# A 31-tap convolution shared between four engines: three channel chunks regrouped by token phase and summed on TensorE with block matrices of 16 taps

## What is computed

```python
def conv_mixer(h, w_pw1, b_pw1, w_dw, b_dw, ln_g, ln_b, w_pw2, b_pw2):
    a = h @ w_pw1 + b_pw1
    u = a[..., :D_MODEL] * jax.nn.sigmoid(a[..., D_MODEL:])
    u = causal_depthwise_conv(u, w_dw) + b_dw          # 31 taps, each channel by itself
    u = jax.nn.silu(layernorm(u, ln_g, ln_b))          # mean and variance over the 1024 channels
    return u @ w_pw2 + b_pw2
```

## Time and profile before

| | |
|---|---|
| Median of three executions | 1853.35 us |
| Profiled execution, its own time | 1847.57 us |
| Its span in the profile | 1845.5 us |
| Mean granted TensorE clock | 0.998 of full speed |
| Convolution: end of pw1 on TensorE | 733.3 us |
| Mean product complete, VectorE centres | 781.4 us |

### The profile page before, as it was taken

One profiled execution on the slowest core, in us unless ns is written; L12 is line 12 of the kernel. 1 busy time (PEld: TensorE's weight loads), 2 busy tenths in 40 slices (PEclk: granted clock), 3 DMA queues, 4 the chain that ended last, 5 costly groups with the idle time before them and its releaser, 6 DMA issues.

```text
span 1845.5 us, 20405 instructions
## 1 busy us (share of the span) xinstructions
PE 1803.3 (98%) x8026; PEld 1445.9 (78%) x8026; DVE 811.9 (44%) x1361; ACT 756.0 (41%) x1199; POOL 780.8 (42%) x360
## 2 busy tenths in 40 slices
PE   7999989999999999999999999999999999999998
PEld 6887768888888877478888888877877888767787
DVE  3794442210121179842210121187868841337733
ACT  4523344322242356454322232355546432444533
POOL 3343224444444369924444444344535543433221
PEclk9999999999999999999999999999999999999999
DMA  5232112323333332012333333333323332232111
GB/s 190 81 102 70 58 36 90 102 93 102 92 102 92 92 103 92 12 46 82 102 101 100 94 98 97 103 103 91 103 80 92 103 96 87 76 92 80 47 46 46
DMA packets 100384, 160.32 MB, mean 87 GB/s; under 512 B 7329, under 2 KB 30497, under 8 KB 100289
## 3 DMA queue, kind: packets, MB, share of 16 engines
q1 hardware_dynamic: 100288, 159.02, 28.3%
HBM read 156.90 MB, written 2.10 MB: 86 GB/s over the span
## 4 chain that ended last, share of the span: by engine, by line
PE 92%; DVE 5%; ACT 2%; issue 1%; DMA 0%; SPq 0%; DVEq 0%; ACTq 0%
PE bank L600 27%; PE bank L602 27%; PE bank L601 27%; PE bank L857 2%; PE bank L901 1%; PE bank L1023 1%; PE bank L682 1%; PE bank L1057 1%; ACT prob L1271 1%; PE bank L1042 1%; PE bank L791 1%; ACT spare L1177 1%; DVE rg_u L2033 0%; PE bank L773 0%; PE bank L999 0%
## 5 line engine op out<-in xcount | busy, mean ns | idle before, releaser
L2385 POOL TENSOR_TENSOR w_lo<-w_raw,w_hi 128x1024 fp32r<-128x1024 f32 (+1 forms) x286 | 694.1, 2431 | 1016.0 <-ACT w_hi L1148 1016.0
L1148 ACT ACTIVATE w_hi<-w_raw 128x1024 fp32r<-128x1024 f32 (+1 forms) x286 | 300.5, 1054 | 593.2 <-PE bank L602 587.5
L600 PE MATMUL bank<-x_hi,w_hi 128*128 128x512 f32 (+1 forms) x1264 | 504.0, 399 | 1.2 <-ACT q_feat L1279 0.8
L602 PE MATMUL bank<-x_hi,w_lo 128*128 128x512 f32 (+1 forms) x1264 | 492.5, 390 | 0.0
L601 PE MATMUL bank<-x_lo,w_hi 128*128 128x512 f32 (+1 forms) x1264 | 492.1, 389 | 0.0
L600 PEld LDWEIGHTS bank<-x_hi,w_hi 128*128 128x128 f32 (+1 forms) x1264 | 236.5, 187 | 59.3 <-issue 10.6
L601 PEld LDWEIGHTS bank<-x_lo,w_hi 128*128 128x128 f32 (+1 forms) x1264 | 236.5, 187 | 53.5 <-issue 4.8
L602 PEld LDWEIGHTS bank<-x_hi,w_lo 128*128 128x128 f32 (+1 forms) x1264 | 236.3, 187 | 51.3 <-issue 0.2
L600 PE MATMUL bank<-w_hi,f_hi 128*128 128x512 f32 x512 | 200.0, 391 | 0.0
L602 PE MATMUL bank<-w_hi,f_lo 128*128 128x512 f32 x512 | 199.3, 389 | 0.0
L601 PE MATMUL bank<-w_lo,f_hi 128*128 128x512 f32 x512 | 199.2, 389 | 0.0
(11 more groups left out here) (298 smaller groups left out, 2124.7 us busy)
## 6 DMA issues: line engine op xcount, KB each, us to landing
w_raw<-in_mlp_w SPq DMA_DIRECT2D x128, 512.0 KB, 3.7
w_raw<-in_even_w_in SPq DMA_DIRECT2D x48, 512.0 KB, 3.8
w_raw<-in_dsa_w_in SPq DMA_DIRECT2D x28, 512.0 KB, 3.6
w_raw<-in_odd_w_in SPq DMA_DIRECT2D x24, 512.0 KB, 3.6
w_raw<-in_conv_w_pw SPq DMA_DIRECT2D x32, 256.0 KB, 3.0
w_raw<-in_even_w_out SPq DMA_DIRECT2D x16, 512.0 KB, 3.8
w_raw<-in_dsa_w_out SPq DMA_DIRECT2D x8, 512.0 KB, 3.8
w_raw<-in_conv_w_pw SPq DMA_DIRECT2D x8, 512.0 KB, 3.8
```

What stands on the lines that cost most here:

```text
L600: e.matmul(o, sh, mh, start=first, stop=False)
L602: m = e.matmul(o, sl, mh, start=False, stop=last)
L1148: e.activation(hi, src, ACT.Copy).then_inc(*w_hi.up(u))
L2385: e.tensor_tensor(lo, src, hi.bitcast(F32), ALU.subtract).then_inc(*w_lo.up(u))
```

## The change

Chunks 4, 5 and 6 are now convolved on TensorE in another form, and no diagonals are made.
- **Phases.** For these chunks VectorE writes u ordered by phase: tokens 0, 4, 8, ... first, then 1, 5, 9, ... SP copies 32 channels of one phase at a time within SBUF, so that one tile (`u4`) has 32 channels in 4 phases on its 128 partitions and 128 columns of tokens: 16 DMAs a chunk of 32 partitions by 512 bytes.
- **Block matrices.** `toep` holds for each of the 12 groups (3 chunks by 4 groups of 32 channels) nine matrices of 128x128. A matrix joins 4 input phases to 4 output phases: 16 taps of one channel block. They are products of two broadcast operands, 1152 elements wide: the mask of equal channels and the shifted weights (`lag_w`). VectorE builds eight (five during the first MLP, three ahead of step 0 of pw1), GpSimd four (steps 0 and 1).
- **TensorE.** A group is nine float32 matmuls of 128 columns into bank 6 or 7 in turn, copied with the bias by ScalarE. These copies stand behind all of its products for chunk 1 and a table load. SP brings each group back by four DMAs into `cc`, still ordered by phase.
- **The others.** VectorE has chunks 0, 2, 3 and 7 whole (124 taps); 7 is split over both sums, as 0 is. GpSimd keeps chunk 1 and then sums chunks 0 to 3 into one tile, so that the mean is five matmuls: chunks 4 and 5, the sum, 7, and 6 last. Readers of chunks 4 to 6 put the tokens back in order by strides.
- **Small loads.** 20 DMAs after the load of the units for q0 bring shifted weights, biases and the mask. A memset at the start clears `lag_w`.

```diff
-PE_TAPS = {6: CONV_TAPS[14:], 7: CONV_TAPS}
-POOL_TAPS = {1: CONV_TAPS, 3: CONV_TAPS[12:]}
-DVE_TAPS = {0: CONV_TAPS, 2: CONV_TAPS, 3: CONV_TAPS[:12], 4: CONV_TAPS, 5: CONV_TAPS, 6: CONV_TAPS[:14]}
+PE_CHUNKS = [4, 5, 6]
+PHASES = 4
+BLOCK = P // PHASES
+SHIFTS = (CONV_W - 1 + PHASES - 1) // PHASES + 1
+PH_LEN = S // PHASES
+PE_GROUPS = [(k, g) for k in PE_CHUNKS for g in range(PHASES)]
+TOEP_POOL = [(4, g) for g in range(PHASES)]
+TOEP_EARLY = [(6, 0), (6, 1), (6, 2), (6, 3), (5, 3)]
+TOEP_DVE = TOEP_EARLY + [(5, 0), (5, 1), (5, 2)]
+POOL_TAPS = {1: CONV_TAPS}
+DVE_TAPS = {0: CONV_TAPS, 2: CONV_TAPS, 3: CONV_TAPS, 7: CONV_TAPS}
-MEAN_ORDER = [0, 2, 1, 4, 5, 6, 3, 7]
+MEAN_ORDER = [0, 2, 1, 3, 4, 5, 7, 6]
...
+        def build_toeplitz(e, k, g):
+            n = PE_CHUNKS.index(k)
+            return e.tensor_tensor(toep[:, n, g], same_ch[:, :].unsqueeze(1).broadcast_to([P, SHIFTS * PHASES, BLOCK]),
+                                   lag_w[:, n, g].unsqueeze(2).broadcast_to([P, SHIFTS * PHASES, BLOCK]), ALU.mult)
```

TensorE's program after pw1:

```diff
-            for k, b in TAP_BANK.items():
+            for k, g in PE_GROUPS:
+                b, n = PHASE_BANKS[g % 2], PE_CHUNKS.index(k)
                 empty(b)
+                w.wait_ge(*phases_in(k))
+                w.wait_ge(*(part_added if (k, g) in TOEP_POOL else dve_tapped).at(k, g))
+                for d in range(SHIFTS):
+                    m = e.matmul(bank[b][:, 0:PH_LEN], toep[:, n, g, d * PHASES:(d + 1) * PHASES, :],
+                                 u4[:, n, g, d:d + PH_LEN], start=d == 0, stop=d == SHIFTS - 1)
+                m.then_inc(*mean_mm.up(k, g))
+                free[b] = cent_sq.at(k, g)
```

ScalarE's, behind the products and the table load:

```diff
+            for k, g in PE_GROUPS:
+                w.wait_ge(*mean_mm.at(k, g))
+                e.activation(cu[:, k, g * PH_LEN:(g + 1) * PH_LEN], bank[PHASE_BANKS[g % 2]][:, 0:PH_LEN], ACT.Identity,
+                             bias=ph_bias[:, g, k - PE_CHUNKS[0]:k - PE_CHUNKS[0] + 1]).then_inc(*cent_sq.up(k, g))
```

SP's queue:

```diff
             up_to("pw10")
             load_gain_row("b_pw2")
+            for n, k in enumerate(PE_CHUNKS):
+                load_to(UNITS[f"pw1{k + 1}"][0] + AHEAD + RAW + 2)
+                w.wait_ge(*u_out.at(k))
+                if n:
+                    w.wait_ge(*phases_in(k - 1))
+                for g in range(PHASES):
+                    for i in range(PHASES):
+                        e.dma_start(u4[i * BLOCK:(i + 1) * BLOCK, n, g, SHIFTS - 1:],
+                                    cu[g * BLOCK:(g + 1) * BLOCK, k, i * PH_LEN:(i + 1) * PH_LEN]
+                                    ).then_inc(*turned_in[0].up("phases", k, PHASES * g + i))
+            w.wait_ge(*phases_in(6))
+            for k, g in PE_GROUPS:
+                if (k, g) == (6, 0):
+                    w.wait_ge(*back_in(4))
+                w.wait_ge(*cent_sq.at(k, g))
+                for j in range(PHASES):
+                    to = PHASES - 1 - j
+                    e.dma_start(cc[g * BLOCK:(g + 1) * BLOCK, k, to * PH_LEN:(to + 1) * PH_LEN],
+                                cu[j * BLOCK:(j + 1) * BLOCK, k, g * PH_LEN:(g + 1) * PH_LEN]).then_inc(*turned_in[k == 5].up("back", k, PHASES * g + j))
```

GpSimd's, behind the adds for chunk 1:

```diff
+            w.wait_ge(*dve_tapped.at(2))
+            e.tensor_tensor(csum[:, :], cc[:, 0, :], cc[:, 2, :], ALU.add).then_inc(*part_added.up("sum", 2))
...
+            e.tensor_tensor(csum[:, :], csum[:, :], cc[:, 1, :], ALU.add).then_inc(*part_added.up("sum", 1))
...
+            e.tensor_tensor(csum[:, :], csum[:, :], cc[:, 3, :], ALU.add).then_inc(*part_added.up("sum", 3))
```

More of the change, by code:

```diff
@@ L470, in build, with phases_in, back_in @@
         part_out = signal("conv_product_made", [(k, i) for k in POOL_TAPS for i in POOL_TAPS[k]])
-        part_added = signal("conv_product_added", POOL_ADDS)
-        diag_out = signal("conv_diag_made", [(k, i) for k in PE_TAPS for i in PE_TAPS[k]])
-        pe_tapped = signal("conv_taps_product", [6, 7])
-        dve_tapped = signal("conv_taps_summed", [0, 3, 2, 4, 5, 6])
-        act_tapped = signal("conv_taps_copied", [7])
-        mean_mm = signal("conv_mean_product", ["mean", "var"])
+        lag_in = signal("conv_lags_landed", range(PHASES * (len(PE_CHUNKS) + 2)), 16)
+        part_added = signal("conv_made_on_gpsimd", TOEP_POOL + POOL_ADDS + [("sum", 2), ("sum", 1), ("sum", 3)])
+        dve_tapped = signal("conv_toeplitz_then_taps_made", TOEP_DVE + [0, 2, 3, 7])
+        turned_in = [signal(f"conv_turned_landed{n}",
+                            [(w, k, i) for w, k in keys for i in range(PHASES * PHASES)], 16)
+                     for n, keys in enumerate(([("phases", k) for k in PE_CHUNKS] + [("back", 4), ("back", 6)], [("back", 5)]))]
+        def phases_in(k):
+            return turned_in[0].at("phases", k, PHASES * PHASES - 1)
+        def back_in(k):
+            return turned_in[k == 5].at("back", k, PHASES * PHASES - 1)
+        mean_mm = signal("conv_phases_and_moments_product", PE_GROUPS + ["mean", "var"])
         var_root = signal("conv_root_taken", ["root"])
         cent = signal("conv_centred", MEAN_ORDER)
-        cent_sq = signal("conv_squared", MEAN_ORDER)
+        cent_sq = signal("conv_phases_copied_then_squared", PE_GROUPS + MEAN_ORDER)
         sq_used = signal("conv_square_used", MEAN_ORDER[:-1])
@@ L1728, in vector_program @@
             e.memset(epsc[:, :], EPS).then_inc(*eps_set.up("eps"))
+            e.memset(lag_w[:, :, :, :], 0.0).then_inc(*eps_set.up("lags"))
             w.wait_ge(*vec_in.last())
@@ L1891, in mlp @@
                                             ALU.subtract).then_inc(*f_lo.up(layer, half, k))
+                        if layer == 0 and early:
+                            w.wait_ge(*lag_in.last())
+                            w.wait_ge(*done("dsa_out1"))
+                            k, part = early.pop(0)
+                            build_toeplitz(e, k, part).then_inc(*dve_tapped.up(k, part))
                     for m in range(2):
@@ L1900, in mlp @@
                         add_tiles(BANKS[name], done(name), updated, n + 1, m, n=m, scale=n)
+            early = list(TOEP_EARLY)
             mlp(0)
@@ L1908, in vector_program @@
             diagonals(1, stat(2, 2))
+            w.wait_ge(*done("down011"))
+            ph_padded = own_dve.after(e.memset(u4[:, :, :, 0:SHIFTS - 1], 0.0))
+            for k, g in TOEP_DVE[len(TOEP_EARLY):]:
+                build_toeplitz(e, k, g).then_inc(*dve_tapped.up(k, g))
             jobs, lanes, lane_mark, turn, side_done = [], [None, None], [None, None], [0], []
+            SPLIT, odd_side = (0, 7), {}
             def add_job(k):
-                if k == 0:
-                    jobs.extend([(0, DVE_TAPS[0][0::2]), (0, DVE_TAPS[0][1::2])])
+                if k in SPLIT:
+                    jobs.extend([(k, DVE_TAPS[k][0::2]), (k, DVE_TAPS[k][1::2])])
                 else:
@@ L1936, in tap @@
                     m = e.tensor_scalar(total, src, weight, V("dw_b", k), ALU.mult, ALU.add)
-                elif k == 0 and i == 1:
+                elif k in SPLIT and i == 1:
                     m = e.tensor_scalar(total, src, weight, None, ALU.mult)
                 else:
-                    dst = total if taps or (k == 0 and i % 2) else cc[:, k, :]
+                    dst = total if taps or (k in SPLIT and i % 2) else cc[:, k, :]
                     m = e.scalar_tensor_tensor(out=dst, in0=src, scalar=weight, in1=total, op0=ALU.mult, op1=ALU.add)
@@ L2439, in add_product @@
                 added[0] += 1
-            due, added = [], [0]
+            due, added, builds = [], [0], list(TOEP_POOL)
             for g in range(KD):
@@ L2449, in gpsimd_program @@
                             split_to(u + AHEAD)
+                            if builds:
+                                w.wait_ge(*lag_in.last())
+                                w.wait_ge(*done("down011"))
+                                c, part_of_c = builds.pop(0)
+                                build_toeplitz(e, c, part_of_c).then_inc(*part_added.up(c, part_of_c))
                         k += 1
```

129 lines of the change are left out of this document (75 added, 54 removed).

## The result

The change makes the kernel slower. The changed kernel has a median of 1857.06 us (1856.17 to 1859.87, 5 runs), the kernel before, run beside it, 1849.39 (1847.45 to 1853.8). The ratio is 1.0045, with a 95% interval from 1.0033 to 1.0057: 7.7 us more, where the forecast had 7.5 less. It lies above the forecast range, and above the bound of 0.3%.

The account below looks back on a forecast made before the run. TensorE, busy 98% of the span, was taken as the bound. Copies ending at 769.5 and the last DMAs back landing at 773.0 put centring at 773.9 instead of 781.4: 7.5 us less, 1845.9 us, range 1840.5 to 1855.

Parts of the forecast that it names:

- SP's issue pace: On SP's queue, each of the 16 KB DMAs within SBUF was to start 0.47 us after the one before.
- the three outs: Dearest back-to-back row for SP's DMA issues: three out in 1.69 us, 0.62 apart, with waits between them.
- a sign of being wrong: On SP's queue in the changed profile, back issues further apart than 0.6 us would show the forecast wrong.
- Landing: Time for a DMA on SP's queue to land: taken as 2.0 us, between rows of 1.8 and 3.5.
- the queue decides: Slower rival on SP's queue: issues 0.62 apart, landing 3.5, centring at 789.5, 8.1 us late, total 1861.4; chance 0.13.
- point of decision: On SP's queue, with landing at 2.0 us, issues about 0.60 us apart are where the change becomes slower.
- the gap: TensorE's wait before its third group, claimed as 8.9 us from 737.4, ending with ScalarE's first copy near 746.3.
- The count of seven products: ScalarE's seventh product after GpSimd's last weight split was to end at 744.5, ahead of table load and copies.
- The clock: TensorE at half clock after its wait: one stretch costs 1.7 us, two 3.4; 2.5 was taken.
- Strides: 512-byte SBUF strides in u, centring and mean products taken at dense cost; dear rival 4.8 us less, 1848.6, chance 0.15.
- Costed at nothing: GpSimd's builds: GpSimd's four matrix builds, 2.7 us each at 648 to 670 between weight splits, were to add no time.
- The reference point: Forecast total of 1845.9 us, set against the 1853.35 median of three runs of the kernel before.

Follow-up runs that it names:

- experiment 3: Changed kernel, but ScalarE copies groups out of the banks in turn with its last products, ahead of its table load: 1855.90 us, ratio 1.0044 to the kernel before.
- Experiment 7: Changed kernel with transposes of a constant filling TensorE's three gaps: 1857.53 us, ratio 1.0044 to the kernel before.
- the dense run: Changed kernel with the 512-byte-stride accesses made dense, tokens of three chunks left in wrong order: 1859.32 us, ratio 1.0052 to the kernel before.
- experiment 5: Changed kernel with chunks 4 and 5 sharing DMAs (64, not 96), early ScalarE copies, two weight loads moved behind the way back: 1838.24 us, ratio 0.9930.
- experiment 9: Kernel of experiment 5 with GpSimd's first build put behind VectorE's four diagonals of the norm: 1835.67 us, ratio 0.9925 to the kernel before.
- experiment 10: Kernel of experiment 9 with ScalarE issuing one of each four DMAs back (8 of 32): 1831.54 us, ratio 0.9912 to the kernel before.
- experiment 4: Changed kernel with ScalarE issuing half the DMAs to phases and a quarter of those back, and copying early: 1845.01 us, ratio 0.9976 to the kernel before.

## Why the prediction was wrong, point by point

- **The step that failed: SP's issue pace.** The prediction took 0.47 us for a DMA within SBUF, from two loads of gla_state, which come from HBM. Within SBUF it is 0.635. The row was not too short, it was of another kind. The 20 small loads of this same change go at 0.475 in a long row, and those of `lag_w` carry 15.5 KB each, nearly the 16 KB of the copies:

```profile
120.86 1.42 SPq L2614 DMA_DIRECT2D conv_lag_weights<-in_vectors  x3
...
130.36 1.36 SPq L2580 DMA_DIRECT2D w_raw<-in_dsa_w_in  x2
```

From the first of the 20 to the load behind them it is 9.5 us (forecast 9.4). So 0.47 was right for loads and wrong for copies within SBUF. The other end of the bound, 0.62 from the three outs, was almost it, and had been set aside as holding waits. The prediction had named back issues further apart than 0.6 as a sign of being wrong.
- **What the step was worth.** With 0.635 us and a landing of 1.8 in the prediction's own sum, each chunk waiting for the one before, centring comes at 784.1 instead of 773.9: 2.7 us late instead of 7.5 early. The pace alone turns the sign.
- **What it did along the chain.** Measured from the last pw1 product, chunk 6's phases start 2.9 us later than forecast, the way back 5.3 later, and it lasts 7.3 longer (32.5 instead of 25.2): 12.6 in all. The last mean product adds 1.2 (2.09 instead of 0.86). With 2.4 us ahead of the stage, and 1.6 behind it that the last row of the table takes back, this is the whole way from 7.5 less to the 8.8 more of the span.
- **Landing** was taken at 2.0 and is 1.8. By the rival "the queue decides" the pace went with a landing of 3.5, and it had centring at 789.5; measured are 790.2. So its mechanism, at 0.13, was the right one. That its number fits to 0.7 us is luck. With the measured pace and landing its sum gives the 784.1 above. The 6 us from there are a queue that starts 2.8 later (720.4), two long issues (2.0) and the dear last product (1.2), and the landing that was too long by 1.7, counted four times, made up for them. Its point of decision, 0.60, fits: 0.635 lies above it, and the kernel is slower.
- **TensorE and ScalarE.** The groups are 2.01 us apart (2.02 forecast), the gap ends with ScalarE's first copy as said, at 749.8 instead of 746.3: the last product ended at 748.0, not at 744.5. The count of seven products was right, but GpSimd's last split starts at 739.5 instead of 735.9, 2.4 of it from the later end of pw1. It cost nothing, as the queue was later still (experiment 3).
- **The clock.** Three stretches instead of one or two, of 10.2, 3.4 and 10.2 us. Experiment 7 took the two long ones away and the stage stayed as it was.
- **Strides.** The dear end was right: 1.18 us against 0.75 for u, 1.03 against 0.68 for the centring, 1.90 against 1.02 for a mean product at full clock. The Trainium skill (SBUF — State Buffer, cachelines) spoke for it, and the dense value was the wrong choice. In the sum it is small: the eight centrings take 5.9 us instead of 4.9, and the dense run's stage is 1.3 shorter.
- **Costed at nothing: GpSimd's builds.** Wrong by 1.24 us. The prediction looked for a late weight split and for slower builds on VectorE, and not for what else VectorE does at that time: small operations that a TensorE product waits for. The Trainium skill (GPSIMD Engine Reference, Key points) says that the two engines contend when VectorE has two SBUF inputs. The 128x4 operation has two, and the trace agrees (1.40 instead of 0.15). The diagonals of L1750, with one tile and a column as scalar, were held too (0.87 to 2.73). The same sentence names a 2-port mode as well; whether the diagonals ran in one, no row shows.
- **VectorE and GpSimd.** Taps done at 763.1 (759.1 forecast), the sum at 755.9 (752.0); neither decided, as said.
- **Behind the stage** the prediction saw no change. It is 1.6 us more up to the last pw2 product: the variance products take 9.33 us instead of 7.67.
- **The reference point.** 1845.9 was set against the median of three runs, 1853.35; in five runs beside the changed kernel it was 1849.4. That moved the forecast by 4 us, but not the sign.

What stays open: what makes an issue within SBUF cost 0.635 us where a small load costs 0.475, and the single long issues. How much of the gain of experiments 5, 9 and 10 belongs to the two weight loads behind the way back, no run shows.

## What to carry to other kernels

Before work moves to another layout, count the DMAs and not the bytes: a row of small ones on one queue goes at a fixed price for each, while their landings overlap. Take that price from DMAs of the same kind, with the same memories as source and target; a long row of loads would have misled here as the short one did. If none exists, let the dear bound decide, for it is multiplied by the count. When the queue is the bound, put more into each DMA first, give a share to a second issuing engine next, and look at what else stands in the queue's order.

## What the runs showed of the hardware

- An issue on SP or ScalarE costs 0.63 to 0.65 us in a steady row within SBUF, on SP at 8, 16 or 32 KB, and each of the two queues keeps its pace while the other issues (experiment 4). Small loads from a kernel input cost 0.475 on SP, and the issue of a 512 KB weight load lasts 0.37. Landing is 1.8 to 1.9 us in the median of most rows. Where both queues sent phases it was 2.3.
- About two issues in a hundred within SBUF last 1.0 to 1.8 us (20 of 976 in the eleven traces, two of 96 in the changed kernel).
- The engine that issues is held, too. While ScalarE sent 8 DMAs it did nothing else for 5.1 us.
- At a stride of 512 bytes in SBUF a float32 product at full clock takes twice as long, a VectorE operation 1.5 to 1.6 times. At half clock the product costs the same, strided or dense (2.09 and 2.08 us).
- An operation of GpSimd beside VectorE can hold up VectorE's tiny ones by more than their own length: 0.15 us became 1.40, and four of 0.87 together became 2.73. In both cases one instruction ended 0.03 to 0.08 us after GpSimd's, and its neighbours kept their length. Moving the build by 2 us moved the loss to the next instruction.
